# Lifting the weight halves of the mixed heads one position earlier, and holding back the weight sums until a reload has landed

## The chip, the core and the metric

The kernel runs as one program on one core of a Trainium2 chip. The metric is the device time of one execution in microseconds (us). The core has five engines that run side by side, each through its own list of instructions in order: PE (TensorE, matmuls), DVE (VectorE), ACT (ScalarE), POOL (GpSimd) and SP (SyncE, which here only issues DMAs). They meet through semaphores. DMAs that SP, ACT and POOL issue all share the core's 16 DMA engines.

## The reference

Two layers, each of this form, for 512 prompt rows and 64 sample rows of width 1024, all in fp32:

```
h = RMSNorm(x)
z = h @ w_in           # [B | C | xin | c_q | c_kv | k_rope | gate_conv | gate_mla]
y_a = B * causal_conv3(C * xin)
y_b = latent attention of 8 heads (q from c_q, keys and values from c_kv, rotary key),
      each 64-row chunk sees its own and earlier chunks; the sample rows see a cache of 512 rows
merged = sigmoid(gate_conv) * y_a + sigmoid(gate_mla) * y_b
x = x + RMSNorm(merged @ w_o)
x = x + RMSNorm(relu(RMSNorm(x) @ w1)^2 @ w2)
```

Outputs are x of both groups and, for each layer, the new latents, rotary keys and convolution tails.

## The kernel before

**Precision.** Every fp32 product is made of three matmuls. An array is split in a high part (ACT copies it to a rounded type, tiles `*_hi`) and a low part (DVE subtracts the high part from the raw array, tiles `*_lo`), and PE adds hi*lo, lo*hi and hi*hi. So each weight that SP loads into a slot (`w_raw`) passes ACT (`pos_hi`, line 1220), then DVE (`pos_lo`, whose subtraction is recorded at line 2071), before PE may use it. Nine slots take 128 x 1024 blocks in turn.

**Heads.** A layer's mixer runs over 8 heads. Each head's work is interleaved on PE: projection blocks of the five weight columns of this head, the small projections of queries, keys and values, the scores, the transposes of the probabilities (`turns`, line 3527), and the product with the values (`attended`). Heads 0, 1 and 7 are plain: five blocks of weight. Heads 2 to 6 are mixed: they use Strassen's scheme in Winograd's form, in which two pairs of blocks are done with seven half-size products each, from sums of weight quarters and sums of the inputs. Such a head takes 8 positions of weight (`HEAD_POS`), named `at` to `at + 7` in the code, where `at` is the head's first. Products 2j and 2j + 1 of a head use position `at + j`; the fourth product pair needs `at + 4`, the products after the transposes need `at + 5` to `at + 7`. In both layers the positions run from 0 to 54, and the first four of w_o follow. The calls `pos_hi(L, at + i)` and `pos_lo(L, at + i)` are written by hand among the other work of ACT and DVE, in rising order of position, once for each position. Indices of 8 and more belong to the next head.

**PSUM.** The products go to four banks in turn (`ring`); PE may fill a bank once what stood in it has been read by DVE or ACT (`ring_free`). DVE forms the outputs of the scheme (`upper_left`, `first_difference`, `second_sum`, `lower_left`, `lower_right`, `upper_right`), ACT reads the first one (`snapshot`). Scores, transposes and attention use the other banks (`att`).

**Attention on ACT and DVE.** After the scores DVE masks and takes row maxima (lines 2404 to 2411), ACT takes exponents (line 1487), DVE divides (line 2429), PE transposes, ACT and DVE split the result into `probs_t_hi` and `probs_t_lo`, and PE multiplies with the values. `small_hi` and `small_lo` split the next head's small weights (`small_raw`), which SP loads once the head's query work is done.

**Weight sums on POOL.** The weight combinations of both layers are made by DMAs alone, in HBM, in the array `weight_sums`: 20 sums, `sums[0]` to `sums[19]`, two for each mixed head of each layer. Head h of layer 0 uses sums 2(h - 2) and 2(h - 2) + 1. `sums_steps` is a pipeline: step n first waits for the copies of sum n and for the additions that steps n - 1 issued, then issues three copies for sum n + 1 (lines 1129 to 1131), two additions for sum n (1135, 1136), one for sum n - 1 (1139) and the last one for sum n - 2 (1142). Steps 0 and 1 come before the rotation of the keys, the others after. SP loads the pieces of a sum into slots; before a head's positions `at + 1` and `at + 5` it waits (`sums_third`) for the last addition of the head's first or second sum. SP is one queue: what stands behind such a wait is issued after it.

**The reload.** Before head 2 the normalised input h, which was stored to HBM during head 1 (`h_store`), is loaded again in four parts (`h_load`, line 958: into `xs_lo_raw`, semaphores `h_landed[0]` to `[3]`), 576 KB each. ACT (`normed_hi`, line 1594) and DVE (`normed_head_lo`) split it in head 2, among the projections.

**Order before.** In a mixed head ACT and DVE split `at + 2` to `at + 4` (head 2: `at + 3`, `at + 4`) before the transposes and `at + 5` to `at + 9` behind them. Plain head 7 begins with two positions (`next_weight(-2)`, `next_weight(-1)`).

## Time and profile before

| | us |
|---|---|
| median of 3 runs | 1723.68 |
| lowest and highest | 1723.24, 1726.3 |
| the profiled execution: its time | 1726.3 |
| the profiled execution: its span | 1724.5 |
| PE busy in the span | 1705.7 |
| DVE busy | 1309.3 |
| ACT busy | 855.1 |

The mean granted clock of TensorE is 0.997 of full speed. The profile is one execution. Its span runs from the first to the last instruction that was recorded; the time of the execution is 1.8 us more. The heads of layer 0 lie between about 50 and 400 us, those of layer 1 between about 900 and 1270 us. PE's matmuls overlap in the trace: one of 288 columns is shown with some 0.29 us and the next starts 0.13 us later. A wait of PE appears as idle time ahead of an instruction, in brackets with what ended it. The order of the instructions says nothing of how long they take; that is read from the trace.

### The profile page before, as it was taken

What the parts mean: (1) busy time and instruction counts of PE and PEld (TensorE: products, weight loads), DVE (VectorE), ACT (ScalarE), POOL (GpSimd) and SP (SyncE); (2) the same over time, 40 slices, a digit from 0 to 9 for tenths busy, and PEclk for the clock granted to TensorE, in tenths of its full rate; (3) what the DMA queues carried; (4) which work ended last, traced back from release to release, by engine and by line L of the source; (5) the groups of instructions that cost most, each with busy time, mean ns of one, the idle gap of its engine ahead of it and who ended that gap; (6) DMA issues with size and microseconds to landing.
All of it is one profiled execution on the core that took longest, in us unless ns stands there. A gap on an engine that the chain in (4) does not pass through costs nothing.

```text
span 1724.5 us, 31894 instructions
## 1 busy us (share of the span) xinstructions
PE 1705.7 (99%) x12735; PEld 1690.9 (98%) x12735; DVE 1309.3 (76%) x2514; ACT 855.1 (50%) x1665; POOL 122.3 (7%) x163
## 2 busy tenths in 40 slices
PE   9999999999999999999999999999999999999997
PEld 9998999999999999999999999999999999999997
DVE  7788787767798786668687797777678887777665
ACT  7625454545465454436366364545435536444452
POOL 1412121212210000000001000000000000000000
PEclk9999999999999999999999999999999999999998
DMA  7899898898762232323124454343532213322231
GB/s 239 198 212 244 214 209 211 178 249 235 163 129 97 89 96 86 99 86 111 60 84 149 148 166 139 114 121 112 171 117 98 99 37 111 98 86 87 74 99 55
DMA packets 90996, 231.54 MB, mean 134 GB/s; under 512 B 9824, under 2 KB 25440, under 8 KB 90848
## 3 DMA queue, kind: packets, MB, share of 16 engines
q1 hardware_dynamic: 71968, 185.45, 33.5%
q0 software_dynamic: 17600, 41.95, 13.8%
q8 instruction: 101, 1.65, 0.4%
q10 hardware_dynamic: 1280, 2.10, 0.3%
q14 instruction: 47, 0.39, 0.1%
HBM read 214.39 MB, written 57.02 MB: 157 GB/s over the span
## 4 chain that ended last, share of the span: by engine, by line
PE 94%; DMA 2%; DVE 2%; ACT 1%; SPq 1%; issue 0%; DVEq 0%; ACTq 0%
PE ring L811 19%; PE ring L813 19%; PE ring L812 19%; PE att L811 11%; PE att L813 11%; PE att L812 11%; PE att L3527 1%; DMA cache_pe_raw<-cache_pe_in 1%; PE att L806 1%; PE att L805 1%; DMA small_raw<-small_in 1%; DMA xs_lo_raw<-h_kept 1%; PE att L818 0%; ACT rope_s L1291 0%; PE att L3343 0%
## 5 line engine op out<-in xcount | busy, mean ns | idle before, releaser
L811 PE MATMUL ring<-xs_hi,w_lo 128*128 128x288 f32 x1872 | 556.6, 297 | 4.3 <-DVE xs_lo L2744 2.2
L813 PE MATMUL ring<-xs_hi,w_hi 128*128 128x288 f32 x1872 | 551.4, 295 | 0.0
L812 PE MATMUL ring<-xs_lo,w_hi 128*128 128x288 f32 x1872 | 551.3, 294 | 0.0
L2071 DVE TENSOR_TENSOR w_lo<-w_raw,w_hi 128x1024 fp32r<-128x1024 f32 (+1 forms) x364 | 370.0, 1035 | 37.3 <-ACT w_hi L1220 27.2
L811 PEld LDWEIGHTS ring<-xs_hi,w_lo 128*128 128x128 f32 x1872 | 351.6, 188 | 7.3 <-DVE ga L2355 2.4
L812 PEld LDWEIGHTS ring<-xs_lo,w_hi 128*128 128x128 f32 x1872 | 351.7, 188 | 1.4
L813 PEld LDWEIGHTS ring<-xs_hi,w_hi 128*128 128x128 f32 x1872 | 351.5, 188 | 0.0
L813 PE MATMUL att<-f_hi,w_hi 128*128 128x288 f32 x960 | 283.2, 295 | 0.0
L812 PE MATMUL att<-f_lo,w_hi 128*128 128x288 f32 x960 | 282.9, 295 | 0.0
L811 PE MATMUL att<-f_hi,w_lo 128*128 128x288 f32 x960 | 282.6, 294 | 0.0
L811 PEld LDWEIGHTS att<-f_hi,w_lo 128*128 128x128 f32 x960 | 180.4, 188 | 0.0
L812 PEld LDWEIGHTS att<-f_lo,w_hi 128*128 128x128 f32 x960 | 180.4, 188 | 0.0
L813 PEld LDWEIGHTS att<-f_hi,w_hi 128*128 128x128 f32 x960 | 180.4, 188 | 0.0
L1212 ACT ACTIVATE w_hi<-w_raw 128x1024 fp32r<-128x1024 f32 x98 | 101.9, 1053 | 87.0 <-DMA w_raw<-blocks_in 86.8
L1220 ACT ACTIVATE w_hi<-w_raw 128x1024 fp32r<-128x1024 f32 x118 | 122.8, 1051 | 7.2 <-DMA w_raw<-blocks_in 6.5
L2923 DVE TENSOR_TENSOR my<-att,my 128x288 f32<-128x288 f32 x160 | 70.8, 451 | 67.7 <-PE att L813 67.7
L813 PE MATMUL ring<-mix_hi,w_hi 128*128 128x288 f32 x384 | 113.5, 295 | 0.0
L811 PE MATMUL ring<-mix_hi,w_lo 128*128 128x288 f32 x384 | 113.1, 295 | 0.0
L812 PE MATMUL ring<-mix_lo,w_hi 128*128 128x288 f32 x360 | 105.9, 294 | 0.0
L811 PE MATMUL ring<-turn_hi,w_lo 128*128 128x288 f32 x320 | 94.9, 296 | 0.0
L812 PE MATMUL ring<-turn_lo,w_hi 128*128 128x288 f32 x320 | 94.4, 295 | 0.0
L813 PE MATMUL ring<-turn_hi,w_hi 128*128 128x288 f32 x320 | 94.2, 295 | 0.0
(342 smaller groups left out, 3184.4 us busy)
## 6 DMA issues: line engine op xcount, KB each, us to landing
w_raw<-blocks_in SPq DMA_DIRECT2D x195, 512.0 KB, 3.7
weight_sums<-blocks_in POOLq DMA_DIRECT2D x80, 256.0 KB, 7.2
w_raw<-blocks_in SPq DMA_DIRECT2D x62, 256.0 KB, 4.6
weight_sums<-blocks_in POOLq DMA_DIRECT2D x20, 512.0 KB, 5.6
weight_sums<-weight_sums POOLq DMA_DIRECT2D x40, 256.0 KB, 7.6
w_raw<-weight_sums SPq DMA_DIRECT2D x20, 512.0 KB, 4.6
w_raw<-weight_sums SPq DMA_DIRECT2D x40, 256.0 KB, 4.4
small_raw<-small_in SPq DMA_DIRECT2D x16, 320.0 KB, 4.6
```

What stands on the lines that cost most here:

```text
L805: pe.matmul(out, both, keys[1], start=False, stop=False)
L806: return pe.matmul(out, both, keys[0], start=False, stop=True)
L811: pe.matmul(out, w[1], x[0], start=first, stop=False)
L812: pe.matmul(out, w[0], x[1], start=False, stop=False)
L813: return pe.matmul(out, w[0], x[0], start=False, stop=last)
L1212: act.activation(hi, raw, ACT.Copy).then_inc(pl.weights_hi, 1)
L1220: act.activation(hi, raw, ACT.Copy).then_inc(pl.weights_hi, 1)
L2071: return dve.tensor_tensor(out, a, hi.bitcast(F32), ALU.subtract)
L2923: dve.tensor_tensor(dst, src, dst, ALU.add).then_inc(pl.w2_free, 1)
L3527: last = pe.transpose(att[:, to:to + P], pl.probs[:, PO[t] + P * j:PO[t] + P * (j + 1)], ident)
```

## The change

It has two parts.

1. POOL's step 5 of the weight sums also waits for the last part of the reload of layer 0 (`h_landed[3]`).
2. ACT and DVE split each weight position of the mixed heads one position earlier in their lists: `at + 3` to `at + 6` ahead of the transposes and `at + 7` to `at + 10` behind them (head 2: `at + 3` to `at + 6` too). Head 7 begins with one position in place of two. On ACT the next head's small weights are also split before the transposed probabilities, not behind the snapshot. The loads and PE's list are as they were.

```diff
-BEFORE_KEYS = 2
+BEFORE_KEYS, AFTER_RELOAD = 2, 5
...
             for n in range(n0, n1):
+                if n == AFTER_RELOAD:
+                    pool.wait_ge(pl.h_landed[3], 16)
                 if n < N_SUMS:
                     pool.wait_ge(pl.sums_copied, 48 * (n + 1))
...
@@ scalar_engine, plain_head (and the same in vector_engine)
                 if h == HEADS - 1:
-                    next_weight(-2)
                     next_weight(-1)
@@ scalar_engine, even_projections
                     if h == FIRST_MIXED:
                         normed_hi(2)
-                    else:
-                        pos_hi(L, at + 3)
                     query_hi(h)
                     rotary_sample(h)
@@ scalar_engine, mixed_head
                     pos_hi(L, at + 3)
                     normed_hi(3)
                     snapshot(0)
+                    pos_hi(L, at + 4)
+                    pos_hi(L, at + 5)
+                    pos_hi(L, at + 6)
                 else:
                     snapshot(0)
-                    pos_hi(L, at + 2)
+                    pos_hi(L, at + 3)
+                    pos_hi(L, at + 4)
                     if h % 2 == 0:
                         even_projections()
                     else:
                         query_hi(h)
-                        pos_hi(L, at + 3)
                         keys_hi(h)
+                    pos_hi(L, at + 5)
+                    pos_hi(L, at + 6)
                 absorbed_hi(h)
-                pos_hi(L, at + 4)
                 eng.wait_ge(pl.conv_in, L * MIXED + h - FIRST_MIXED + 1)
                 apart()
                 conv_begin(h)
                 exponents(h)
-                pos_hi(L, at + 5)
+                pos_hi(L, at + 7)
+                small_hi(L, h + 1)
                 turned_hi(h)
                 snapshot(1)
-                pos_hi(L, at + 6)
-                small_hi(L, h + 1)
-                pos_hi(L, at + 7)
                 pos_hi(L, at + 8)
                 eng.wait_ge(pl.ring_free, freed(L, r_mixed(h, 10)))
                 act.activation(pl.gb[:, cols(0)], pl.gb[:, cols(0)], ACT.Tanh, scale=0.5)
                 pos_hi(L, at + 9)
+                pos_hi(L, at + 10)
@@ vector_engine, mixed_head (heads 3 to 6)
                     upper_left(0, pl.cv[:, cols(0)])
+                    pos_lo(L, at + 3)
                     first_difference(0)
                     second_sum(0)
-                    pos_lo(L, at + 2)
+                    pos_lo(L, at + 4)
...
+                    pos_lo(L, at + 5)
                 conv_state(h)
                 lower_left(0, pl.u[:, 2:2 + NH])
                 conv_first_half()
+                pos_lo(L, at + 6)
                 lower_right(0, pl.v2[:, :])
                 upper_right(0, pl.cv[:, cols(1)])
                 conv_second_half()
-                pos_lo(L, at + 4)
...
-                pos_lo(L, at + 5)
+                pos_lo(L, at + 7)
...
                 turned_lo(h)
-                pos_lo(L, at + 6)
                 small_lo(h + 1)
                 upper_left(1, pl.gb[:, cols(0)])
+                pos_lo(L, at + 8)
                 first_difference(1)
-                pos_lo(L, at + 7)
                 second_sum(1)
-                pos_lo(L, at + 8)
+                pos_lo(L, at + 9)
                 lower_left(1, pl.ga[:, cols(0)])
-                pos_lo(L, at + 9)
+                pos_lo(L, at + 10)
```

POOL at the start of step 5 after the change; in brackets the semaphores that an instruction waits for:

```order
L1139 DMA weight_sums<-weight_sums 128x512
L1142 DMA weight_sums<-weight_sums 128x512
L1129 DMA weight_sums<-blocks_in 128x2x512 [waits sums_second,sums_first,sums_third,sums_copied,h_landed3]
L1130 DMA weight_sums<-blocks_in 128x512
L1131 DMA weight_sums<-blocks_in 128x512
```

Nothing has moved; `h_landed3` is new in the third row, and all later weight sums stand behind it.

ACT in head 6 of layer 0 before, from the splitting of the values to the weight behind the exponents (`w_hi` is a weight position, `slot` names where it lies, `q_abs_hi` is the absorbed query, `probs,rs` the exponents):

```order
L1456 ACTIVATE v_hi<-att 128x512 [waits projected] x2
L1220 ACTIVATE w_hi<-w_raw 128x1024 [waits slot1]
L1448 ACTIVATE q<-att 128x288 [waits projected] x2
L1476 ACTIVATE q_pe_sample<-q_pe_84 128x64 [waits latents_stored,rope_lo]
L1476 ACTIVATE q_pe_sample<-q_pe_85 128x64
L1482 ACTIVATE q_abs_hi<-att 128x2x64 [waits absorbed]
L1220 ACTIVATE w_hi<-w_raw 128x1024 [waits slot2]
L1498 ACTIVATE conv_tail<-u 128x4 [waits conv_in]
L1499 ACTIVATE cv<-u,consts 128x578
L1487 ACTIVATE probs,rs<-att,nmx,rows 128x128 [waits row_max]
```

And the same stretch of ACT after the change (its line numbers are two higher):

```order
L1458 ACTIVATE v_hi<-att 128x512 [waits projected] x2
L1450 ACTIVATE q<-att 128x288 [waits projected] x2
L1478 ACTIVATE q_pe_sample<-q_pe_84 128x64 [waits latents_stored,rope_lo]
L1478 ACTIVATE q_pe_sample<-q_pe_85 128x64
L1222 ACTIVATE w_hi<-w_raw 128x1024 [waits slot3]
L1222 ACTIVATE w_hi<-w_raw 128x1024 [waits slot0]
L1484 ACTIVATE q_abs_hi<-att 128x2x64 [waits absorbed]
L1500 ACTIVATE conv_tail<-u 128x4 [waits conv_in]
L1501 ACTIVATE cv<-u,consts 128x578
L1489 ACTIVATE probs,rs<-att,nmx,rows 128x128 [waits row_max]
```

Slots 3 and 0 hold positions `at + 5` and `at + 6` of head 6 (47 and 48 of the layer). Their high parts now stand ahead of the absorbed query and the exponents; before, they stood behind the exponents and behind the transposed probabilities.

DVE in the same head, before, from the queries to the row maxima (`u`, `cv` and `head_v` hold the outputs of the scheme and the convolution):

```order
L2071 TENSOR_TENSOR q<-att,q 128x288 [waits proj_hi] x2
L2437 MEMSET u 128x2
L2438 COPY u<-consts 128x2
L2628 TENSOR_TENSOR u<-ring,head_v_108 128x288 [waits ring_free,ring_full]
L2643 TENSOR_TENSOR u<-u,cv 128x288 [waits ring_free]
L2632 TENSOR_TENSOR head_v_108<-ring,head_v_108 128x288 [waits ring_full]
L2634 TENSOR_TENSOR head_v_107<-head_v_107,ring 128x288 [waits dve_own]
L2639 TENSOR_TENSOR cv<-head_v_107,ring 128x288 [waits ring_free,ring_full]
L2647 TENSOR_TENSOR u<-head_v_108,cv 128x224 [waits ring_free]
L2648 TENSOR_TENSOR u<-head_v_108,cv 128x64
L2071 TENSOR_TENSOR w_lo<-w_raw,w_hi 128x1024 [waits weights_hi]
L2404 MEMSET att 64x64 [waits scored] x4
```

DVE there after the change:

```order
L2073 TENSOR_TENSOR w_lo<-w_raw,w_hi 128x1024 [waits weights_hi]
L2439 MEMSET u 128x2
L2440 COPY u<-consts 128x2
L2629 TENSOR_TENSOR u<-ring,head_v_108 128x288 [waits ring_free,ring_full]
L2644 TENSOR_TENSOR u<-u,cv 128x288 [waits ring_free]
L2073 TENSOR_TENSOR w_lo<-w_raw,w_hi 128x1024 [waits weights_hi]
L2633 TENSOR_TENSOR head_v_108<-ring,head_v_108 128x288 [waits ring_full]
L2635 TENSOR_TENSOR head_v_107<-head_v_107,ring 128x288 [waits dve_own]
L2640 TENSOR_TENSOR cv<-head_v_107,ring 128x288 [waits ring_free,ring_full]
L2648 TENSOR_TENSOR u<-head_v_108,cv 128x224 [waits ring_free]
L2649 TENSOR_TENSOR u<-head_v_108,cv 128x64
L2406 MEMSET att 64x64 [waits scored] x4
```

The low part directly ahead of the row maxima is gone; those of positions 47 and 48 now stand ahead of the convolution's first and second half.

## Rows read from the trace of the kernel before

**Rows 1.** The page's first part: busy us, share and instructions of each engine.

```profile
PE 1705.7 (99%) x12735; PEld 1690.9 (98%) x12735; DVE 1309.3 (76%) x2514; ACT 855.1 (50%) x1665; POOL 122.3 (7%) x163
```

**Rows 2.** What PE waited for: us in total, times, longest.

```profile
PE att L811 <- DVE probs_t_lo L2071: 2.4, 1, 2.4
PE ring L811 <- DVE xs_lo L2744: 2.2, 1, 2.2
...
PE att L811 <- DVE k_lo L2071: 0.7, 1, 0.7
PE ring L811 <- DVE xs_lo L2071: 0.7, 2, 0.4
PE att L811 <- DVE rx L2454: 0.6, 1, 0.6
```

**Rows 3.** Chain that ended last: start, us, what; the cache load of head 7.

```profile
378.11 12.65 DMA cache_pe_raw<-cache_pe_in
```

**Rows 4.** The reload's tile, layer 0: ns min/median/max, first and last start; landing.

```profile
L958 SPq DMA_DIRECT2D xs_lo_raw<-h_kept x4: 360/439/731, 141.8 to 145.4; - x4
...
DMA to landing us min/median/max: 9.4/12.5/13.4
```

**Rows 5.** The same tile, the four loads of layer 1 (994 to 999 us).

```profile
DMA to landing us min/median/max: 4.6/5.2/6.0
```

**Rows 6.** Timeline of DVE in head 2, layer 0: start, us, what, idle before.

```profile
152.43 1.36 DVE L2071 TENSOR_TENSOR xs_lo<-xs_lo_raw,xs_hi 128x1152 fp32r<-128x1152 f32 x1 [0.50 <-ACT xs_hi L1594]
153.71 0.68 DVE L2071 TENSOR_TENSOR k_lo<-att,k_hi 128x512 fp32r<-128x512 f32 x1
```

**Rows 7.** Timeline of POOL: starts of steps 5, 6 and 12, last addition of step 11.

```profile
137.12 0.75 POOL L1129 DMA_DIRECT2D weight_sums<-blocks_in  x1 [5.96 <-DMA weight_sums<-weight_sums]
...
163.20 0.76 POOL L1129 DMA_DIRECT2D weight_sums<-blocks_in  x1 [6.78 <-DMA weight_sums<-weight_sums]
...
309.99 0.83 POOL L1142 DMA_DIRECT2D weight_sums<-weight_sums  x1 [7.25 <-issue]
316.37 0.75 POOL L1129 DMA_DIRECT2D weight_sums<-blocks_in  x1 [5.55 <-DMA weight_sums<-weight_sums]
```

**Rows 8.** Window of POOL's step 10: us, engines' busy, clock, DMA share, GB/s.

```profile
261.33:289.54 28.21, 28.21 (x210) 27.82 (x209) 20.66 (x37) 11.74 (x18) 5.21 (x8) 1.00 0.87 218
```

**Rows 9.** Timeline of SP's queue: positions 47 and 48 of layer 0.

```profile
317.23 0.35 SPq L954 DMA_DIRECT2D w_raw<-blocks_in  x1
317.63 3.10 SPq L954 DMA_DIRECT2D w_raw<-weight_sums  x2
```

**Rows 10.** The weights' raw tile, SP's four loads from 317 to 321 us.

```profile
DMA to landing us min/median/max: 6.5/7.6/9.6
```

**Rows 11.** Timeline of ACT in head 6, layer 0.

```profile
329.96 0.40 ACT L1476 ACTIVATE q_pe_sample<-q_pe 128x64 fp32r<-128x64 f32 x2
...
342.18 1.06 ACT L1220 ACTIVATE w_hi<-w_raw 128x1024 fp32r<-128x1024 f32 x1
```

**Rows 12.** Timeline of DVE in head 6, layer 0.

```profile
332.89 0.45 DVE L2632 TENSOR_TENSOR head_v<-ring,head_v 128x288 f32<-128x288 f32 x1
...
335.03 0.22 DVE L2648 TENSOR_TENSOR u<-head_v,cv 128x64 f32<-128x64 f32 x1
335.94 1.23 DVE L2071 TENSOR_TENSOR w_lo<-w_raw,w_hi 128x1024 fp32r<-128x1024 f32 x1 [0.70 <-ACT w_hi L1220]
...
337.93 1.61 DVE L2407 TENSOR_REDUCE mx<-att 128x1 f32<-128x128 f32 x4
```

**Rows 13.** Timeline of PE: the transposes of head 6, layer 0.

```profile
344.02 0.82 PE L3527 MATMUL att<-consts,probs 128*128 128x128 f32 x6
```

**Rows 14.** The small weights' raw tile: SP's last loads for head 6 (292.6 us).

```profile
DMA to landing us min/median/max: 9.8/10.2/10.6
```

**Rows 15.** Timeline of ACT in head 5, layer 0.

```profile
301.04 1.36 ACT L1494 ACTIVATE probs_t_hi<-att 128x512 fp32r<-128x512 f32 x3 [2.08 <-PE att L3527]
...
303.88 1.69 ACT L1228 ACTIVATE small_hi<-small_raw 128x1792 fp32r<-128x1792 f32 x1
```

More of the change, by code:

```diff
@@ L2503, in plain_head @@
                 if h == HEADS - 1:
-                    next_weight(-2)
                     next_weight(-1)
@@ L2663, in even_projections @@
                         head_mix_lo(2)
-                    else:
-                        pos_lo(L, at + 3)
                     query_lo(h, 0)
@@ L2676, in mixed_head @@
                     second_sum(0)
+                    pos_lo(L, at + 4)
                     normed_head_lo(3)
+                    pos_lo(L, at + 5)
                 else:
                     upper_left(0, pl.cv[:, cols(0)])
+                    pos_lo(L, at + 3)
                     first_difference(0)
                     second_sum(0)
-                    pos_lo(L, at + 2)
+                    pos_lo(L, at + 4)
                     if h % 2 == 0:
@@ L2687, in mixed_head @@
                         query_lo(h, 1)
-                        pos_lo(L, at + 3)
                         keys_lo(h)
+                    pos_lo(L, at + 5)
                 conv_state(h)
```

## The prediction

> **What bounds the kernel.** I read the page's busy times first, then what PE waited for, then the chain, and last the timelines of POOL, SP, ACT and DVE around the places that the change touches. PE is busy for 1705.7 of 1724.5 us [rows 1], so no more than 18.8 us can be won by any order of work, and a good part of that lies at the very start and end. The list of PE's waits narrows it down: behind the start there are 2.4 us for the transposed probabilities of head 1, 0.6 + 0.7 + one of the two 0.4 at the seam of heads 1 and 2 in layer 0, 2.2 us behind head 7 of layer 0 and the other 0.4 in layer 1 [rows 2]. In heads 3 to 6 of both layers PE never waits for a weight. So the second part of the change, which makes weights ready earlier, has no wait there to remove; what it can do is make something else later. The reader is to see in the rows that PE is served in time everywhere in the mixed heads, and then to ask by how little.
>
> **Part one, the held sums: what it gives.** The four loads of the reload take 9.4 to 13.4 us in layer 0 [rows 4], where POOL's DMAs run beside them, and 4.6 to 6.0 in layer 1, where there are none [rows 5]. With step 5 held, I take layer 1's values for layer 0. What depends on them: DVE was idle for 0.50 us before the first low part of the reload, and this one stood right ahead of the keys' low part, for which PE waited 0.7 [rows 2, 6]. With the load there in time DVE runs through, so PE gets the keys 0.5 us sooner, and the 0.4 us wait behind it moves with it. The 0.6 us before it stems from DVE's backlog behind the 2.4 us wait of head 1, which ends before step 5 starts at 137.12 [rows 7]: neither is touched. Gain: 0.5 us (bounds: 0, and 0.7 + 0.4 = 1.1 if both waits went).
>
> The Trainium skill, page "DMA: Bandwidth & Descriptors", section "Queues, rings and completion order", says that each DMA engine goes round the queues that have work, a packet at a time, so an empty POOL queue leaves every turn to SP. By that rule, the trace agrees: medians of 12.5 against 5.2 us.
>
> **Part one, what it costs.** The last of the four loads is issued at 145.4 [rows 4]; with 5.8 us to its landing, near layer 1's 6.0 [rows 5], it is there at 151.2. Step 5, at 137.12 before, starts 14.1 us late. POOL is a serial chain of such steps: from step 5's start at 137.12 to step 12's at 316.37 there are 7 of them, 25.6 us each [rows 7], the slowest, step 10, with 28.2 us and the DMA engines 0.87 busy [rows 8]. So all later sums come late, and the one to ask for is the last of layer 0, that of head 6. Its last addition was issued at 309.99 and had landed shortly before step 12 began at 316.37, some 315.8; SP issued position 47, which waits for it, at 317.23 [rows 7, 9]. That is a margin of 1.4 us, against a delay of 14.1.
>
> Does the delay stay 14.1? Step 5 used to run with the reload beside it and will now run behind it, so it may be 1 to 2 us shorter than its 26.1; the rest meets the same mean load. I take 12 and keep 14.1, and 0 to 17 as ends (0: each of the seven steps 2 us shorter; 17: one more of them as slow as step 10). With 12 the last addition lands at 327.8.
>
> **Part two, what then waits.** Positions 47 and 48 (both behind that addition in SP's queue, 4 pieces) were issued over 317.2 to 320.8 and took 6.5 to 9.6 us [rows 9, 10]. Issued all at once from 327.8, over 1.3 us, the last one lands 9.5 us behind the addition (8.9 by the median, 10.9 by the longest), at 337.3. In the old order this would have been harmless: ACT took position 47 at 342.18 [rows 11]. In the new order ACT comes to 47 and 48 when the sample's queries are done, at 330.4 [rows 11], and stands there until 337.3. Behind it on ACT wait the absorbed query, the convolution's start and the exponents; DVE waits for the same high parts ahead of both halves of the convolution and the row maxima; PE waits for the probabilities to transpose. From the landing of 48 the chain is: high part 1.06 [rows 11]; low part 1.23; lower right to the end of the convolution's second half 2.4 (332.89 to 335.25); masks 0.2; row maxima to transposes 6.1 (337.93 to 344.02) [rows 12, 13]. That is 11.0 us, so the transposes start at 348.3, where they started at 344.02: 4.3 us late. PE has no work of its own left in its list before them, and having no slack afterwards it does not make this up. The 0.5 us won in head 2 is inside this number, since POOL's dates are absolute: the wait grows by what PE was early.
>
> The break-even follows: the addition has to land by 344.0 - 11.0 - 9.5 = 323.5, a delay of 7.7 us.
>
> **Part two, the rest.** The mixed heads' lists hold as many splits as before, one moved from behind the transposes to ahead of them; ACT (855 us busy) and DVE (1309) have idle stretches in both halves [rows 1], so at layer 1, without POOL, I price it at nothing. Its bounds: a low part of 1.23 us uncovered in each of ten heads is 12 us lost, and the other way no more than the 0.4 of layer 1 is won. I take zero, for the low part straight ahead of the row maxima [rows 12] is gone at the place where DVE is latest. Head 7 starts with one split less; its 2.2 us wait hangs on the cache load of 12.65 us [rows 3], so this wins nothing. The small weights' high part is now ahead of the transposed probabilities: head 6's, issued at 292.6, took 10.6 us [rows 14] to 303.2, while ACT began head 5's probabilities at 301.04; with 1.69 for the high part itself [rows 15] they would start at 304.9, 3.9 us late. PE had no wait there, so part of this is hidden by a distance that no row gives, and 12 us later POOL's copies no longer start just ahead of that load. I price it at nothing and keep 3.9 as the other end.
>
> **Sum.** +4.3 us. The profiled execution took 1726.3 (span 1724.5 and 1.8 around it), which by itself would go to 1730.6; it is the highest of the three runs, and the median 1723.68 goes to 1728.0.
>
> **Rivals.**
> 1. *The delay is absorbed.* Were POOL held up mainly by SP's loads, a lighter 137 to 160 us would let it catch up below 7.7 us of delay. For it: steps differ by some us with the load. Against: none of the in-head steps is short enough alone. Then only the gain stays: -0.5, 1723.2. Not slower.
> 2. *The last wait shrinks.* The 2.2 us behind head 7 hangs on a load slowed by POOL's DMAs [rows 2, 3]; a new phase of POOL can let it through. With all three waits at the seam gone as well: -(0.6 + 0.7 + 0.4 + 2.2) = -3.9, and 1719.8. Against it: POOL's DMAs are present all the time there, only shifted.
> 3. *The delay is kept in full.* By the nearest rows it is 14.1; the addition lands at 329.9, with the longest landing of 10.9 the transposes start at 351.8: +7.8, 1731.5. With the small weights' 3.9 on top it is 1735.4, the far end. The rule of the Trainium skill above ("DMA: Bandwidth & Descriptors", section "Queues, rings and completion order") speaks for this one: if each busy queue gets its turn whatever the other holds, less traffic from SP shortens POOL's steps little.
> 4. *The wait does nothing*: the load lands before 137.12. Excluded by its issue at 141 us.
>
> **Chances.** Forecast (+1.5 to +7) 0.43; absorbed 0.27; last wait shrinks 0.08; kept in full or worse 0.22. A measurement of this kernel can tell about 0.2% (3.4 us) from no change. Slower by more takes two thirds of the forecast's share and nearly all of the last one: 0.49. Within: the rest of the forecast, all of the absorbed and part of the second: 0.44. Faster: 0.07, the second. For 8 in 10 the range reaches from just under the absorbed case to a little over the third rival: 1722.0 to 1733.0.
>
> **What would show it.** Right: POOL's step 5 starts near 151; the reload lands in 5 to 6 us; in head 6 of layer 0 SP issues position 47 only behind POOL's last addition, near 328; ACT is idle for some 7 us before a weight's high part there; PE has a new wait of about 4 us before the transposes, named by the probabilities. Wrong: that addition lands before 323.5, or PE waits elsewhere, above all before the product with the values in heads 3 and 5, or POOL's steps behind 151 take under 24 us.

## The result, and the profile after

The changed kernel takes 1735.9 us (median of 6 runs, 1732.8 to 1743.0), beside 1725.0 for the kernel before (6 runs, 1723.2 to 1726.5). The ratio is 1.0075, 95% interval 1.0052 to 1.0096. That is slower by 10.9 us, above the 1733 at which the prediction's range ended. One run of the kernel before, beside the experiments below, took 3383.5 us and is in no ratio. The profiled execution took 1734.1 us, its span is 1732.3.

The page's busy times, as in [rows 1]:

```profile
PE 1708.8 (99%) x12735; PEld 1693.2 (98%) x12735; DVE 1309.6 (76%) x2514; ACT 857.6 (50%) x1665; POOL 122.2 (7%) x163
```

No engine has more instructions than before. What PE waited for, as in [rows 2] (us in total, times, longest):

```profile
PE att L3528 <- DVE probs L2431: 6.3, 3, 2.4
PE att L811 <- DVE probs_t_lo L2073: 2.4, 2, 1.7
...
PE ring L811 <- DVE xs_lo L2092: 1.1, 1, 1.1
PE ring L811 <- DVE xs_lo L2745: 0.9, 1, 0.9
PE ring L811 <- DVE xs_lo L2073: 0.7, 2, 0.4
```

The first row is new: three waits for the probabilities ahead of the transposes. The prediction expected one such wait, in head 6. None of the three is there: they stand in head 2 of layer 0, in head 7 of layer 0 and in head 2 of layer 1.

Both kernels issue the same 12,735 matmuls in the same order, so the start of the n-th in one trace can be set against the n-th in the other, and the difference read off stretch by stretch. Here in us, against the profile before; the stretches are by the time before. Each row is one execution. The other kernels are explained below.

| | 0-170 | head 2, 170-182 | heads 2-6, 182-376 | head 7, 376-398 | behind it, 398-411 | head 2 of layer 1, 1018-1034 | rest | sum |
|---|---|---|---|---|---|---|---|---|
| changed kernel | -2.2 | +3.7 | +2.0 | +4.1 | -1.3 | +2.1 | -0.6 | +7.9 |
| the same, again | +1.0 | +2.1 | 0.0 | +0.2 | +3.8 | +2.1 | -0.4 | +8.8 |
| hold only | +0.3 | 0.0 | -0.1 | 0.0 | -1.0 | 0.0 | +0.6 | -0.2 |
| order only | +0.4 | +3.7 | +1.3 | +1.3 | +3.4 | +3.7 | -0.5 | +13.2 |
| head 2 back | -2.1 | 0.0 | 0.0 | +1.2 | +4.6 | 0.0 | -0.5 | +3.2 |
| three places back | -0.4 | 0.0 | +4.7 | +0.7 | +2.2 | 0.0 | -0.1 | +7.1 |
| three back, no hold | -0.6 | 0.0 | +4.0 | 0.0 | +2.3 | 0.0 | -0.4 | +5.3 |
| head 6 back too | +0.9 | 0.0 | +1.0 | 0.0 | +1.4 | 0.0 | +0.1 | +3.4 |
| the same, again | -0.6 | 0.0 | +4.4 | 0.0 | 0.0 | 0.0 | -0.5 | +3.3 |
| heads 5, 6 back | -1.2 | 0.0 | +0.6 | 0.0 | +4.6 | 0.0 | -0.5 | +3.5 |
| all heads back | 0.0 | 0.0 | +0.1 | 0.0 | -1.6 | 0.0 | -0.5 | -2.0 |
| changed, longer hold | -0.5 | +3.7 | +15.9 | +0.4 | +3.7 | +3.8 | -0.4 | +26.6 |
| before, longer hold | -0.4 | 0.0 | +13.4 | +2.6 | -2.4 | 0.0 | +0.6 | +13.7 |

The two columns of head 2 are 0.0 wherever head 2's list is the old one, and some 2.1 or 3.7 wherever it is the new one; the other columns of layer 0 change from one execution to the next. Some of these executions are far from their kernel's median: those of "order only", "three back, no hold" and "changed, longer hold" were the slowest of their runs, and that of "all heads back" was 5 us below its median.

**Head 2.** DVE ahead of the row maxima in layer 0, first the kernel before, then the changed one (start, us, what, idle before in brackets):

```profile
169.30 0.39 DVE L2647 TENSOR_TENSOR u<-head_v,cv 128x224 f32<-128x224 f32 x1
...
169.75 1.22 DVE L2071 TENSOR_TENSOR w_lo<-w_raw,w_hi 128x1024 fp32r<-128x1024 f32 x1
170.97 0.46 DVE L2404 MEMSET att<- 64x64 f32 x4
```

```profile
160.24 1.23 DVE L2073 TENSOR_TENSOR w_lo<-w_raw,w_hi 128x1024 fp32r<-128x1024 f32 x1
...
163.37 1.22 DVE L2073 TENSOR_TENSOR w_lo<-w_raw,w_hi 128x1024 fp32r<-128x1024 f32 x1
...
165.78 1.23 DVE L2073 TENSOR_TENSOR w_lo<-w_raw,w_hi 128x1024 fp32r<-128x1024 f32 x1
...
167.86 1.22 DVE L2073 TENSOR_TENSOR w_lo<-w_raw,w_hi 128x1024 fp32r<-128x1024 f32 x1
169.00 0.45 DVE L2633 TENSOR_TENSOR head_v<-ring,head_v 128x288 f32<-128x288 f32 x1
...
171.06 0.33 DVE L2406 MEMSET att<- 64x64 f32 x4
```

There is no bracket in this stretch: DVE does not rest for more than 0.1 us. Four low parts of 1.22 us stand ahead of the row maxima where two stood. PE had come here 2.2 us early (its waits in head 1 and for the keys were shorter in this execution) and got nothing for it: the row maxima begin at the same 171.3. In layer 1 the trace has the same picture, four low parts where two stood. What PE did then (matmuls, idle before in brackets):

```profile
177.38 1.31 PE L3528 MATMUL att<-consts,probs 128*128 128x128 f32 x10 [1.98 <-DVE probs L2431]
...
178.79 0.44 PE L813 MATMUL ring<-xs_hi,w_hi 128*128 128x288 f32 x1
179.03 0.44 PE L811 MATMUL ring<-xs_hi,w_lo 128*128 128x288 f32 x1
179.27 0.44 PE L812 MATMUL ring<-xs_lo,w_hi 128*128 128x288 f32 x1
```

The matmuls of 288 columns behind the wait start 0.24 us apart and not 0.13. The windows of this stretch name the reason (us, busy times of PE, weight load, DVE, ACT, POOL, then the granted clock):

```profile
177.00:180.00 3.00, 2.62 (x18) 2.63 (x19) 2.89 (x7) 1.72 (x4) 0.41 (x1) 0.80 0.99 188
180.00:183.00 3.00, 3.00 (x17) 3.00 (x17) 1.97 (x4) 1.44 (x3) 0.00 (x0) 0.64 0.88 214
183.00:186.00 3.00, 3.00 (x21) 2.87 (x21) 2.05 (x3) 1.40 (x2) 0.00 (x0) 1.00 1.08 235
```

Shortly behind the wait the clock fell from 2.4 to 1.2 GHz, by these windows for some 3.4 us, which cost 1.5 us more. The Trainium skill, page "TensorE: Matmul & The Clock Gate", section "Part 1: The HAM clock gate", says that the gate knows only these two rates; by the pitch of 0.24 against 0.13 us, the trace agrees.

**The reload and POOL.** The reload, as in [rows 4], and the starts of POOL's steps 5 and 12, as in [rows 7]:

```profile
L958 SPq DMA_DIRECT2D xs_lo_raw<-h_kept x4: 359/440/509, 140.2 to 143.8; - x4
...
DMA to landing us min/median/max: 4.4/5.0/5.8
```

```profile
149.75 0.75 POOL L1129 DMA_DIRECT2D weight_sums<-blocks_in  x1 [28.02 <-DMA xs_lo_raw<-h_kept]
...
318.12 0.75 POOL L1129 DMA_DIRECT2D weight_sums<-blocks_in  x1 [5.39 <-DMA weight_sums<-weight_sums]
```

Step 5 starts 12.6 us later than before, step 12 only 1.8. By the profile alone the delay has vanished; the experiments say otherwise. The last addition landed at 317.5, SP issued position 47 at 322.40 without waiting for it, and ACT took the positions 47 and 48 one behind the other, with no idle time before them:

```profile
333.67 1.99 ACT L1222 ACTIVATE w_hi<-w_raw 128x1024 fp32r<-128x1024 f32 x2
```

So the chain on which the forecast rested did not occur in this execution.

**Heads 5 to 7.** ACT in the changed kernel: head 5, and the end of head 6 with the start of head 7.

```profile
305.03 1.70 ACT L1230 ACTIVATE small_hi<-small_raw 128x1792 fp32r<-128x1792 f32 x1 [4.61 <-DMA small_raw<-small_in]
306.64 1.34 ACT L1496 ACTIVATE probs_t_hi<-att 128x512 fp32r<-128x512 f32 x3
...
354.82 1.06 ACT L1222 ACTIVATE w_hi<-w_raw 128x1024 fp32r<-128x1024 f32 x1 [4.04 <-DMA w_raw<-blocks_in]
...
359.92 1.06 ACT L1222 ACTIVATE w_hi<-w_raw 128x1024 fp32r<-128x1024 f32 x1 [3.71 <-DMA w_raw<-blocks_in]
362.10 1.06 ACT L1222 ACTIVATE w_hi<-w_raw 128x1024 fp32r<-128x1024 f32 x1 [1.11 <-DMA w_raw<-blocks_in]
365.31 0.69 ACT L1647 ACTIVATE ga<-ga 128x576 f32<-128x576 f32 x1 [2.15 <-DVE head_v L2635]
...
382.24 1.06 ACT L1222 ACTIVATE w_hi<-w_raw 128x1024 fp32r<-128x1024 f32 x1 [2.70 <-DMA w_raw<-blocks_in]
```

In head 5 ACT stood 4.61 us for the small weights with the transposed probabilities behind them: PE +1.9. At the end of head 6 it stood 8.9 us for three raw weights; DVE's outputs and the merge of head 6 stood behind them, SP stored that merged head at 368.38 (before 361.34) and issued the first block of w_o, which waits for the store, at 374.28 (before 366.94). ACT met that late block in head 7, ahead of the exponents, and PE lost 2.4 us before the transposes and the clock with it: +4.1. The general picture is one row, ACT's splits of the weights between 140 and 350 us: count, busy us and mean ns, then the idle us ahead of them. Before, then changed:

```profile
L1220 ACT ACTIVATE w_hi<-w_raw 128x1024 fp32r<-128x1024 f32 x38 | 39.6, 1053 | 0.6 <-DMA w_raw<-weight_sums 0.6
```

```profile
L1222 ACT ACTIVATE w_hi<-w_raw 128x1024 fp32r<-128x1024 f32 x37 | 38.5, 1057 | 16.6 <-DMA w_raw<-blocks_in 9.4 <-DMA w_raw<-weight_sums 7.2
```

Before, the list came to nearly every weight when it had landed. Now it comes to some of them before the landing and stands, with work for PE behind it: in this execution to 8 of the 37, for 0.8 to 3.3 us each. How long varies: a second profiled execution of the changed kernel has 28.0 us there. This time is not itself a loss, for PE loses only what goes beyond its own slack.

### The profile page after: what moved, and what is told of

It reads as the page before. It is cut to its first block, busy times and chain, and to the rows that moved or that the text cites. A ratio compares the mean times of both kernels' runs of the same rounds, so it can differ in the third digit from the quotient of the medians.

```text
span 1732.3 us, 31894 instructions
## 1 busy us (share of the span) xinstructions
PE 1708.8 (99%) x12735; PEld 1693.2 (98%) x12735; DVE 1309.6 (76%) x2514; ACT 857.6 (50%) x1665; POOL 122.2 (7%) x163
## 4 chain that ended last, share of the span: by engine, by line
PE 90%; DVE 5%; DMA 3%; ACT 1%; issue 1%; SPq 0%; DVEq 0%; ACTq 0%
PE ring L811 18%; PE ring L813 18%; PE ring L812 18%; PE att L811 11%; PE att L813 11%; PE att L812 11%; DMA w_raw<-blocks_in 1%; DMA small_raw<-small_in 1%; PE att L3528 1%; DVE w_lo L2073 1%; PE att L806 1%; PE att L805 1%; DVE xs_lo L2073 0%; ACT probs L1489 0%; DVE turn_lo L2073 0%
## 5 line engine op out<-in xcount | busy, mean ns | idle before, releaser
L2073 DVE TENSOR_TENSOR w_lo<-w_raw,w_hi 128x1024 fp32r<-128x1024 f32 (+1 forms) x364 | 370.8, 1038 | 35.7 <-ACT w_hi L1222 26.6
```

The costliest lines, as they stand in the source:

```text
L2073: return dve.tensor_tensor(out, a, hi.bitcast(F32), ALU.subtract)
```

## Experiments: the two parts apart, and head 2

The kernel before ran beside each; its medians were 1724.8 to 1726.6, its other single runs 1721.5 to 1733.1.

**Hold only.** The kernel before, with

```diff
+                if n == AFTER_RELOAD:
+                    pool.wait_ge(pl.h_landed[3], 16)
```

> The kernel before with the held step 5 of the weight sums alone; the order of the splits is the old one. Theory L (the lists: the loss comes from splits that stand ahead of something PE waits for, in head 2 of both layers, in head 5 and at the end of head 6): no loss without them, 1723.5 to 1725.5, and the reload's gain of 0.5 us at most. Rival H (the hold: later weight sums make the loads late): slower by 4 us or more, with PE waits in heads 5 to 7 of layer 0. In the trace: last addition of layer 0's last sum lands 1 to 4 us later than the 315.8 of before, not 12, by both, since the changed kernel showed 317.5.

Measured: 1725.0 us, ratio 0.9996 (95% interval 0.9985 to 1.0007, as all that follow). The hold costs nothing with the old order, and gives nothing. The reason is not that POOL caught up: step 5 started at 152.98 and step 12 here

```profile
328.81 0.75 POOL L1129 DMA_DIRECT2D weight_sums<-blocks_in  x1 [4.60 <-DMA weight_sums<-weight_sums]
```

12.4 us later than before. SP itself stood for POOL's last additions; what it waited for them between 140 and 420 us (in total, times, longest):

```profile
SPq L944 <- DMA weight_sums<-weight_sums: 37.4, 5, 11.4
```

In the kernel before it never waited for them. So the loads were late and the old order had the slack for it. ACT took position 47 at 342.30, unhurried, as the prediction had said of the old order. The part of the expectation that the sum would land 1 to 4 us late was wrong.

**Order only.** The changed kernel without those two lines.

> The changed kernel without the held step. Theory L: as slow as the changed kernel within 2 us, 1733 to 1738, with the wait of about 2.2 us before the transposes of head 2 in layer 0 and in layer 1. Rival H, and the forecast's own mechanism (positions 47 and 48 late behind POOL): 1724 to 1726, as the kernel before.

Measured: 1736.7 us, ratio 1.0062 (1.0043 to 1.0080), as theory L had it. The loss is in the order; whether the hold adds to it in the changed kernel (1.0075, 1.0052 to 1.0096) can't be told from these two. PE's waits:

```profile
PE att L3526 <- DVE probs L2429: 4.3, 3, 1.9
PE att L811 <- DVE probs_t_lo L2071: 3.1, 2, 2.1
PE ring L811 <- DVE xs_lo L2743: 2.9, 1, 2.9
```

In head 2 this execution lost 3.7 us in either layer, wait and low clock together (table). Step 12 started at 305.9 and no wait in head 6 hangs on POOL: the forecast's mechanism isn't needed for the loss.

**Head 2 back.** The changed kernel with head 2's list as before, on ACT and in the same way on DVE:

```diff
@@ ACT, head 2
-                    pos_hi(L, at + 4)
-                    pos_hi(L, at + 5)
-                    pos_hi(L, at + 6)
...
                 absorbed_hi(h)
+                if h == FIRST_MIXED:
+                    pos_hi(L, at + 4)
...
-                pos_hi(L, at + 7)
+                pos_hi(L, at + (5 if h == FIRST_MIXED else 7))
...
                 snapshot(1)
+                if h == FIRST_MIXED:
+                    pos_hi(L, at + 6)
+                    pos_hi(L, at + 7)
```

> The changed kernel with head 2's list as before (two splits ahead of the transposes, not four). Theory L: the two waits of 2.2 us before head 2's transposes go, and with the first also the 1.5 us in which PE ran at half clock behind it: 5.8 us less than the changed kernel, so near 1730. Rival (a full DVE is not the cause, PE only waits there because it is early): no change, 1736.

Measured: 1731.1 us, ratio 1.0028 (1.0013 to 1.0043); both columns of head 2 are 0.0. Against order only that is 5.6 us less, against the changed kernel 4.8 by the medians and 8 by the ratios (other runs). The rival of an early PE falls: here PE came to head 2 2.1 us early and did not wait, and in the second profiled execution of the changed kernel it came 1.0 us late and did. Shown: the two more splits in head 2's list, on a DVE without idle time, cost 2.1 us of wait in each layer, 3.7 where the clock falls too.

**Three places back.** Besides head 2, the next head's small weights go behind `snapshot(1)` again, and the last split of head 6 (`at + 10`) goes back to the start of head 7 (on DVE too).

```diff
-                small_hi(L, h + 1)
                 turned_hi(h)
                 snapshot(1)
+                small_hi(L, h + 1)
...
-                pos_hi(L, at + 10)
+                if h < HEADS - 2:
+                    pos_hi(L, at + 10)
...
                 if h == HEADS - 1:
+                    next_weight(-2)
                     next_weight(-1)
```

> The changed kernel with three places as before: head 2's list, the next head's small weights behind the snapshot, and the last split of head 6 left to head 7. The hold and the order of heads 3 to 6 stay. Theory L: the time of the kernel before, 1723 to 1726. Rival O (the order of heads 3 to 6 itself costs, or the hold): 1729 or more.

Measured: 1730.7 us, ratio 1.0032 (1.0008 to 1.0055), single runs 1722.4 to 1746.1. Theory L's number fell: some 5 us are left, and the small weights and the last split together show no effect beside head 2 back (1.0028). And here the forecast's own mechanism shows. SP, ACT and PE in head 6:

```profile
326.07 0.33 SPq L954 DMA_DIRECT2D w_raw<-blocks_in  x1
326.44 0.91 SPq L954 DMA_DIRECT2D w_raw<-weight_sums  x2
```

```profile
337.70 1.06 ACT L1222 ACTIVATE w_hi<-w_raw 128x1024 fp32r<-128x1024 f32 x1 [3.92 <-DMA w_raw<-blocks_in]
```

```profile
348.25 1.31 PE L3539 MATMUL att<-consts,probs 128*128 128x128 f32 x10 [1.54 <-DVE probs L2435]
```

SP stood for POOL's last addition until 326.0, ACT stood for the landing of position 48 until 337.7, the transposes began 10.6 us behind that at 348.25. Only 1.8 of the 4.7 us that heads 2 to 6 lost in this execution fell there; 2.1 fell before, at the start of head 6, where PE waited 1.7 us for the rope's sums behind a weight with no late sum.

## Experiments: what is left, and its dose

**Three back, no hold.** The same kernel without the hold:

```diff
-                if n == AFTER_RELOAD:
-                    pool.wait_ge(pl.h_landed[3], 16)
```

> The previous kernel (head 2, small weights and last split as before) without the held step. Theory P (what is left there is the forecast's own mechanism: where POOL's last sum of layer 0 lands near 326, ACT stands for positions 47 and 48 in head 6 of layer 0): without the hold that sum lands near 315 or earlier, ACT does not stand longer than 2 us and the time is that of the kernel before, 0.999 to 1.001. Rival O (the order of heads 3 to 6 costs by itself): 1.002 or more, with PE waits in heads 3 to 7 that do not hang on POOL.

Measured: 1728.2 us, ratio 1.0005 (0.9993 to 1.0017). Theory P's number came, but not its account: the trace, of the slowest of the 12 runs, still has waits at the start and the end of head 6, for the rope's sums (1.9 us) and an output of the scheme (1.3), behind ACT standing for raw weights that have nothing to do with POOL's last sum. ACT's row, as above:

```profile
L1220 ACT ACTIVATE w_hi<-w_raw 128x1024 fp32r<-128x1024 f32 x38 | 39.4, 1054 | 19.1 <-DMA w_raw<-weight_sums 11.1 <-DMA w_raw<-blocks_in 8.0
```

ACT stands as long as in the changed kernel's profile (16.6), and the median is not shown to be above that of the kernel before.

**Head 6 back too.** With the hold, but `at + 5` and `at + 6` of head 6 behind the exponents and the transposed probabilities, on DVE likewise:

```diff
-                    pos_hi(L, at + 5)
-                    pos_hi(L, at + 6)
+                    if h < HEADS - 2:
+                        pos_hi(L, at + 5)
+                        pos_hi(L, at + 6)
...
-                pos_hi(L, at + (5 if h == FIRST_MIXED else 7))
+                pos_hi(L, at + (5 if h in (FIRST_MIXED, HEADS - 2) else 7))
...
```

> The same kernel with the held step, but with the splits of positions 47 and 48 (and of at + 5, at + 6 of head 6 in layer 1) behind the transposes, where they were before. Theory P: time of the kernel before, 0.999 to 1.001, even where the last sum lands at 326 or 328. Rival O: 1.002 or more as in the run with three places as before.

Measured: 1732.1 us, ratio 1.0035 (1.0019 to 1.0051). Theory P fell as the cause of the rest: the positions 47 and 48 can't meet the late sum here, and the loss is as large. A second profiled execution of the same kernel:

> The kernel with head 6 back, a second look: its profiled execution before was 3 us faster than its median. Both: no wait before head 2's transposes. Theory I: PE waits in heads 3 to 5, behind loads of weight sums. Rival J: waits at the ends of heads, named by merged heads or stores, or only the wait behind head 7 grows.

It took 1729.4 us and lost 4.4 us in heads 2 to 6, nearly all at one place, here on ACT and PE at the start of head 6:

```profile
321.87 1.06 ACT L1222 ACTIVATE w_hi<-w_raw 128x1024 fp32r<-128x1024 f32 x1 [5.61 <-DMA w_raw<-blocks_in]
323.42 1.06 ACT L1222 ACTIVATE w_hi<-w_raw 128x1024 fp32r<-128x1024 f32 x1 [0.49 <-DMA w_raw<-blocks_in]
324.51 3.30 ACT L1293 ACTIVATE rope_s<-att 32x288 f32<-32x288 f32 x8
```

```profile
327.62 0.41 PE L811 MATMUL att<-small_hi,ckv_lo 128*128 128x256 f32 x1 [2.71 <-DVE rope_t L2396]
```

The first weight is `at + 3`. Its halves were issued at 310.2 and 310.6, and the second landed 11.2 us later. In the kernel before the same load landed at 318.0, and ACT came to it only at 328.41, behind the rope: 10 us of slack that the new order has spent.

**Heads 5 and 6 back; all heads back.** `at + 5` and `at + 6` behind the transposes in head 5 as well, then in all mixed heads:

```diff
-                    if h < HEADS - 2:
+                    if h < HEADS - 3:
                         pos_hi(L, at + 5)
                         pos_hi(L, at + 6)
```

```diff
-                    if h < HEADS - 2:
-                        pos_hi(L, at + 5)
-                        pos_hi(L, at + 6)
...
-                pos_hi(L, at + (5 if h in (FIRST_MIXED, HEADS - 2) else 7))
+                pos_hi(L, at + 5)
```

> The kernel with head 2, small weights, last split and head 6 as before, and now head 5's at + 5 and at + 6 behind the transposes too; hold kept. Theory I (with the held sums, a split that stands ahead of the transposes meets its load late in every head whose second sum comes near its need; with the longer hold head 5 was the worst): 2 to 4 us less than with head 5 early, 1.000 to 1.002 of before. Rival J (the remaining 5 us come from the extra split at the end of heads 2 to 5, at + 10, and from later stores): no change against that kernel, 1.0025 or more.

> The same with at + 5 and at + 6 behind the transposes in all five mixed heads; what is left of the change is the hold, at + 3 and at + 4 ahead of the projections, and at + 10 at the end of heads 2 to 5. Theory I: the time of the kernel before, 0.999 to 1.001. Rival J: 1.0025 or more.

Measured: 1729.8 us, ratio 1.0030 (1.0015 to 1.0045), and 1729.2 us, 1.0014 (1.0000 to 1.0028). Neither theory holds as put: head 5 by itself gives nothing that can be seen, all heads together perhaps half of the rest, and the intervals overlap, so even that half is not shown. ACT's row in the last one:

```profile
L1222 ACT ACTIVATE w_hi<-w_raw 128x1024 fp32r<-128x1024 f32 x38 | 38.8, 1053 | 7.6 <-DMA w_raw<-blocks_in 3.9 <-DMA w_raw<-weight_sums 3.8
```

**The longer hold.** The wait is for the last low part of the reload, in the changed kernel and in the one before.

```diff
-                    pool.wait_ge(pl.h_landed[3], 16)
+                    pool.wait_ge(pl.h_lo, 4)
```

> The changed kernel, with step 5 held until the last low part of the reload is made (near 166) and not until its landing (near 151): the dose of the delay is 15 us larger. Theory P (the forecast's chain works whenever the last sum is late): step 5 starts at 166, the last sum of layer 0 lands at 332 to 343, SP issues position 47 right behind it, ACT stands for positions 47 and 48, and head 6's transposes start 20.5 us behind that landing (9.5 for the loads, 11.0 for the chain); 3 to 12 us more than the changed kernel's 1735.9. Rival C (POOL catches up, so its phase does not matter): the changed kernel's time.

> The kernel before with the same longer hold. By the forecast's break-even for the old order (ACT takes position 47 at 342.2, its loads take up to 9.5, so the sum has to land by 332.7) the loss is what the sum lands beyond 332.7: 0 to 10 us, and at least 3 us less than the changed kernel loses against its own short hold. Rival C: no loss.

Measured: 1749.0 us, ratio 1.0125 (1.0100 to 1.0149), and 1740.7 us, 1.0085 (1.0064 to 1.0107). Step 5 started at 167.87 and 166.80, step 12 at 342.32 and 344.12. What PE waited for between 140 and 350 us, new order and old order:

```profile
PE att L3528 <- DVE probs L2431: 12.0, 3, 7.9
PE att L811 <- DVE rope_t L2391: 1.8, 2, 1.5
```

```profile
PE ring L811 <- DVE w_lo L2073: 8.4, 2, 6.0
```

So POOL's phase is kept. The longer hold cost the new order 13 us more by the medians and 9 by the ratios, where 3 to 12 were expected; it cost the old order 15 to 16, where 0 to 10 were expected and the old order was to be the cheaper.

The place, too, is not the forecast's: head 6's transposes have no wait of PE in either trace. SP stood for each sum, and for head 5's second one until 289.4 in the new order and 293.6 in the old; of the four pieces then issued the last landed after 12.1 and 12.0 us (behind layer 0's last sum it was 9.0 and 9.4). In the new order ACT stood 7.4 us for that weight ahead of the exponents of head 5, and PE 7.9 (the rest of the 12.0 is in heads 2 and 4). In the old order PE waited 2.4 us for that weight itself, and 6.0 us a little later, when ACT had stood 6.4 us for head 6's small weights: SP had issued them behind the sum, and they landed after up to 14.1 us. Why these loads were slower than those behind the last sum is not shown. By its margin that sum was not the one to fear: in the kernel before it had landed when the next step of POOL began at 261.33, and SP issued the weight behind it at 275.07.

**The changed kernel again.** No edit.

> The changed kernel itself, a second look. The two waits before head 2's transposes (2 us or more, layers 0 and 1) are the same; the waits of heads 5 and 7 of layer 0 need not be, if they hang on how long a load takes in this execution.

1734.9 us. Head 2 lost 2.1 us in either layer (the clock stayed up), heads 5 and 7 lost nothing, and the wait behind head 7 was 4.7 us instead of 0.9:

```profile
PE ring L811 <- DVE xs_lo L2745: 4.7, 1, 4.7
PE att L3528 <- DVE probs L2431: 3.8, 2, 1.9
```

**Small weights.** The kernel before with the small weights ahead of the transposed probabilities in the mixed heads, and its mirror in the plain heads:

```diff
@@ mixed_head, ACT
+                small_hi(L, h + 1)
                 turned_hi(h)
                 snapshot(1)
                 pos_hi(L, at + 6)
-                small_hi(L, h + 1)
```

```diff
@@ plain_head, ACT
-                small_hi(L, h + 1)
                 turned_hi(h)
+                small_hi(L, h + 1)
```

> The kernel before with one change: in the mixed heads ACT splits the next head's small weights ahead of the transposed probabilities. Theory S (this edit is one of the costs): 1 to 3 us more, with PE waits for probs_t_lo in head 3 or 5 of layer 0, and none in layer 1. The forecast's price: nothing.

> The kernel before with the mirror of that edit: in the plain heads, where the small weights' split stands ahead of the transposed probabilities, it goes behind them. In head 1 of layer 0 ACT stood 6.9 us for those weights and PE 2.4 us for the transposed probabilities. Theory S: that 2.4 us wait goes, and half of it or more stays won: 1 to 2.5 us less than before. Rival (whatever PE wins there it loses at the next place where DVE is full, head 2): no change.

Measured: 1724.9 us, ratio 1.0001 (0.9987 to 1.0015), and 1724.5 us, 0.9994 (0.9983 to 1.0006). Alone the first costs nothing that can be measured. The mirror removes the 2.4 us wait of head 1 [rows 2]. PE's waits from 120 to 200 us are then

```profile
PE att L811 <- DVE rx L2454: 1.1, 1, 1.1
PE ring L811 <- DVE xs_lo L2071: 0.3, 1, 0.3
```

and still the time moves by less than the measurement can tell. The interval allows a gain of up to 2.9 us, and in this profile the span is 1.9 us shorter, so theory S isn't excluded either.

**Hold and late small weights together.** The kernel before with the two lines of the hold and the edit just shown in the plain heads.

> The kernel before with the short hold and, in the plain heads, the small weights split behind the transposed probabilities: the two edits that cost nothing. Theory S: head 1's wait of 2.4 us is gone and the reload is early, 0.9985 to 0.9995 of before. Rival: as with the second edit alone, no change that can be measured.

Measured: 1724.3 us, ratio 0.9990 (0.9977 to 1.0004), the lowest of all, but not shown to be better than the kernel before.

## Why the prediction was wrong

**The reload (right in size, its gain not shown).** It landed in 4.4 to 5.8 us against 5 to 6 expected, and step 5 started at 149.8 against 151.2. The 0.6 us won at the keys is in traces without the hold too (order only: 0.6), so it belongs to the execution before.

**The direction (right, by luck).** The forecast was slower by 4.3 us, all of it from the chain in head 6. In the changed kernel's profile that chain is absent: the last addition landed at 317.5, ahead of the break-even of 323.5, which the prediction itself had named as a sign of being wrong.

**The delay of 12 us (right, but set on one execution).** The start of step 12 in five traces without the hold: 316.4, 305.9, 309.9, 305.3, 309.2, mean 309.34. In ten with it: 318.1, 321.6, 328.8, 317.3, 326.6, 322.1, 325.8, 324.4, 319.0, 318.1, mean 322.17. That is 12.8 us, from a start that is 14.5 later (137.1 to 151.6, same traces); the seven steps are 1.6 us shorter in all. The Trainium skill, page "DMA: Bandwidth & Descriptors", section "Queues, rings and completion order", which the prediction took to speak for a delay kept in full, says only that a DMA engine goes round the queues that have work; by that, an empty SP queue would leave its turns to POOL, so the rule does not speak for that rival. No run here tells why the steps keep their length. But 316.37 [rows 7] was the latest of the five. Set on the mean, the last addition lands near 321.5, short of the break-even of 323.5, so the chain bites in some executions only. The changed kernel's two profiled executions are of the other sort: step 12 began at 318.1 and 321.6. Rival 1 (the delay is absorbed), which the changed kernel's profile seems to show, is wrong.

**The chain in head 6 (right where it happens).** With three places back the addition landed at 326.0. The prediction's 9.5 and 11.0 us give 346.5; measured 348.25, 11.7 and 10.6, with a wait of PE of 1.54 us. It is not where the changed kernel loses: its transposes of head 6 started 3.5 us later than before, nearly all of it from earlier heads.

**"The rest" (the step that failed).** The prediction wrote that the lists hold as many splits as before, one moved, and priced this at nothing. In head 2 two moved ahead of the transposes (two stood there before, four now), and DVE is full there. The price was 0, with 12 as the other end for ten heads, and the reason given was read in head 6 [rows 12]. Measured are 2.1 to 3.7 in each layer for head 2: 5.8 in the profile, whose total is 7.9, and 4.8 of the 10.9 by the medians or 8 by the ratios (head 2 back beside the changed kernel). [rows 6] showed two of DVE's instructions back to back in that head, and the same timeline has no idle time of more than 0.1 us from there to the row maxima. The ends were kept for the range, but the low clock and both layers of head 2 together were given no case of their own.

**The small weights (nothing, with 3.9 as the other end).** 1.9 us in the profile, none in the second profiled execution, nothing alone.

**What no step had.** The prediction asked of two positions whether they have landed when ACT comes, and not of the others. The new order comes to some of them too early (8 of 37 in the profile, up to 3.3 us, and 9 of 38 in the second one, up to 6.0; 16.6 and 28.0 us of standing against 0.6). And it priced a wait of PE at its length: behind waits of 1.9 us or more the clock fell in several traces, for 1.1 to 1.6 us more.

**Open.** It is not shown where the other 3 to 6 us of the loss come from. The hold alone has 0.9996, the order of heads 3 to 6 alone 1.0005 (0.9993 to 1.0017), both 1.0032 (1.0008 to 1.0055). These two intervals overlap; that of both with head 6 back, 1.0035 (1.0019 to 1.0051), lies clear of the order alone. So the two probably act together, and the place changes with each execution (the start of head 6, the end of head 6, the wait behind head 7). SP's own waits for POOL's sums do not give the size: 18.4 us with three places back and 5.2 and 13.2 with head 6 back, but 37.4 in hold only, which lost nothing, and none in the changed kernel's profile. That late sums put POOL's copies beside the loads that ACT now meets unlanded would explain it; it is only argued. Whether the extra split at the ends of heads 2 to 5 has a share was not told apart.

## What to carry to other kernels

Moving a split earlier in an engine's list is free only if its load has landed by then, and if the engine has idle time ahead of the next thing that the bottleneck engine waits for; count the moved instructions head by head, at the seams above all, where the lists differ. A margin read from one execution of a DMA chain is one draw: here it spread over 11 us among five traces, nearly as much as the delay in question, so ask for the price at the mean and at both ends.

## What the runs showed that was not expected

- A PE wait of 1.9 to 3 us costs up to 1.6 us more in clock, but not always. Before head 2's transposes PE waited 1.9 to 2.0 us in both layers of three profiled executions: the clock fell behind it in both layers with order only (granted 0.61), in layer 0 alone in the changed kernel (0.64), and in neither layer in its second execution (1.00). Behind head 1's wait it fell in hold only (2.35 us, 0.50 from 137 to 140 us) and not in the kernel before (2.44 us, 1.00).
- A chain of DMAs that started 14.5 us late on the mean was still 12.8 us late seven steps of some 25 us later, beside loads that vary from 3 to 11 us.
- SP stood 37.4 us in all behind late sums with the old order and the time did not move (0.9996): what a late load costs was set by how early the list asks for it.
- Removing the longest wait of the kernel before (2.4 us in head 1) did not show in the time (0.9994, 0.9983 to 1.0006); its trace gives 1.1 us back at head 7's transposes.
